# Moving the operands of SwiGLU to other offsets in on-chip memory

## The reference, cut to what matters

```
def swiglu(h, w1, w3, w2):            # h: 512 x 1024, w1 and w3: 1024 x 2816, w2: 2816 x 1024
    return (jax.nn.silu(h @ w1) * (h @ w3)) @ w2

for l in range(2):
    x = x + 0.5 * swiglu(rmsnorm(x, g_ffn1[l]), w1_a[l], w3_a[l], w2_a[l])
    x = x + mixers(rmsnorm(x, g_mix[l])) @ w_o[l]
    x = x + 0.5 * swiglu(rmsnorm(x, g_ffn2[l]), w1_b[l], w3_b[l], w2_b[l])
```

## Time and profile before

| | |
|---|---|
| median of three runs | 2801.64 us |
| the profiled execution's own time | 2803.92 us |
| its span, first to last instruction | 2801.9 us |
| TensorE matmuls busy | 2716.1 us (97%), 15,816 matmuls |
| TensorE weight loads busy | 2181.3 us (78%) |
| VectorE busy | 1774.7 us (63%) |
| ScalarE busy | 1092.5 us (39%) |
| GpSimd busy | 416.2 us (15%) |
| mean granted TensorE clock | 0.991 |

### The profile page before, as it was taken

One profiled execution on the slowest core, in us unless ns is written; L12 is line 12 of the kernel. 1 busy time (PEld: TensorE's weight loads), 2 busy tenths in 40 slices (PEclk: granted clock), 3 DMA queues, 4 the chain that ended last, 5 costly groups with the idle time before them and its releaser, 6 DMA issues.

```text
span 2801.9 us, 40254 instructions
## 1 busy us (share of the span) xinstructions
PE 2716.1 (97%) x15816; PEld 2181.3 (78%) x15816; DVE 1774.7 (63%) x2645; ACT 1092.5 (39%) x1586; POOL 416.2 (15%) x464
## 2 busy tenths in 40 slices
PE   9998999889699999999999999999999999999998
PEld 6576343333399998888889999899998888899997
DVE  6635232222787776665588777986777655787775
ACT  6832110100454444332354444554444233354443
POOL 3211000000021111101131110311101111221111
PEclk9999999999899999999999999999999999999999
DMA  5146999999465643332345564456542333365651
GB/s 214 45 175 263 420 420 420 420 420 421 141 181 166 173 136 100 103 101 94 100 124 168 167 172 136 114 164 176 158 136 89 94 94 106 98 172 142 176 158 60
DMA packets 138176, 505.65 MB, mean 180 GB/s; under 512 B 17025, under 2 KB 17537, under 8 KB 113153
## 3 DMA queue, kind: packets, MB, share of 16 engines
q1 hardware_dynamic: 101952, 422.36, 40.4%
q0 software_dynamic: 34688, 73.42, 12.8%
q10 hardware_dynamic: 1344, 7.23, 0.6%
HBM read 502.95 MB, written 4.19 MB: 181 GB/s over the span
## 4 chain that ended last, share of the span: by engine, by line
PE 73%; DMA 14%; DVE 5%; issue 4%; ACT 2%; POOL 1%; SPq 0%; DVEq 0%; ACTq 0%; POOLq 0%
PE bank L658 22%; PE bank L656 22%; PE bank L657 22%; DMA raw_more<-in_moe 4%; DMA raw<-in_moe 3%; PE bank L804 3%; DMA raw_over<-in_moe 3%; PE bank L839 2%; DVE w_lo L1875 1%; DMA sums<-in_w_b 1%; ACT w_hi L1272 1%; PE bank L662 1%; DMA raw<-in_w_b 1%; DVE ft L2289 0%; DMA x_rows<-x_tok 0%
## 5 line engine op out<-in xcount | busy, mean ns | idle before, releaser
L1875 DVE TENSOR_TENSOR w_lo<-raw,w_hi 128x1024 fp32r<-128x1024 f32 (+1 forms) x346 | 434.6, 1269 | 272.2 <-ACT w_hi L1272 265.7
L656 PE MATMUL bank<-xf_hi,w_lo 128*128 128x256 f32 x2112 | 590.1, 279 | 17.2 <-DVE w_lo L1875 9.6
L658 PE MATMUL bank<-xf_hi,w_hi 128*128 128x256 f32 x2112 | 585.3, 277 | 0.0
L657 PE MATMUL bank<-xf_lo,w_hi 128*128 128x256 f32 x2112 | 585.2, 277 | 0.0
L1272 ACT ACTIVATE w_hi<-raw 128x1024 fp32r<-128x1024 f32 (+1 forms) x356 | 366.0, 1039 | 273.9 <-PE bank L658 247.3
L656 PEld LDWEIGHTS bank<-xf_hi,w_lo 128*128 128x128 f32 x2112 | 397.6, 188 | 27.2 <-issue 14.1
L657 PEld LDWEIGHTS bank<-xf_lo,w_hi 128*128 128x128 f32 x2112 | 397.6, 188 | 2.4 <-issue 1.0
L658 PEld LDWEIGHTS bank<-xf_hi,w_hi 128*128 128x128 f32 x2112 | 397.4, 188 | 0.0
L658 PE MATMUL bank<-g_hi,w_hi 128*128 128x512 f32 x832 | 327.4, 394 | 0.0
L657 PE MATMUL bank<-g_lo,w_hi 128*128 128x512 f32 x832 | 326.2, 392 | 0.0
L656 PE MATMUL bank<-g_hi,w_lo 128*128 128x512 f32 x832 | 323.5, 389 | 0.3 <-DVE g_lo L2331 0.3
(11 more groups left out here) (367 smaller groups left out, 4549.0 us busy)
## 6 DMA issues: line engine op xcount, KB each, us to landing
raw_more<-in_moe SPq DMA_DIRECT2D x96, 1024.0 KB, 26.5
raw_over<-in_moe SPq DMA_DIRECT2D x48, 1024.0 KB, 27.4
raw<-in_w_a SPq DMA_DIRECT2D x77, 512.0 KB, 6.1
raw<-in_w_b SPq DMA_DIRECT2D x76, 512.0 KB, 6.3
raw<-in_w_in SPq DMA_DIRECT2D x73, 512.0 KB, 3.6
raw_top<-in_moe SPq DMA_DIRECT2D x24, 1024.0 KB, 27.9
raw<-in_moe SPq DMA_DIRECT2D x24, 1024.0 KB, 28.6
sums<-in_w_a POOLq DMA_DIRECT2D x88, 256.0 KB, 4.9
```

Of the source, the lines that this page charges most:

```text
L656: e.matmul(out, a_lo, b_hi, start=start, stop=False, skip_group_check=partial)
L657: e.matmul(out, a_hi, b_lo, start=False, stop=False, skip_group_check=partial)
L658: return e.matmul(out, a_hi, b_hi, start=False, stop=stop, skip_group_check=partial)
L1875: e.tensor_tensor(lo, source_of(k), hi.bitcast(F32), ALU.subtract).then_inc(s["lo"], 1)
```

## The change

Three pads of 16 values become 64 values, and the pads that follow shrink so that everything else stays where it was. `g` and `xf` move up by 192 bytes, from 192 to 384 past a multiple of 512. `pad_e` is moved from ahead of `e_hi` to behind `e_lo`, so that `e` moves down by 64 bytes, from 192 to 128. `raw_late`, `xT`, `rsq`, `sums`, `uu`, `snap`, `vv`, `ft` and the mixer's own buffers stay. No instruction, wait or DMA is added, removed or reordered, and only start addresses differ.

```
-        sb("pad_g", [P, 16])
+        sb("pad_g", [P, 64])
         g_hi = sb("g_hi", [P, 8, T], F32R)
         g_lo = sb("g_lo", [P, 8, T], F32R)
-        sb("pad_late", [P, 112])
+        sb("pad_late", [P, 64])
...
-            sb("pad_xf", [P, 16], into=ffn)
+            sb("pad_xf", [P, 64], into=ffn)
             xf_hi = sb("xf_hi", [P, KH, 7 * HALF], F32R, ffn)
             xf_lo = sb("xf_lo", [P, KH, 7 * HALF], F32R, ffn)
-            sb("pad_sums", [P, 112], into=ffn)
+            sb("pad_sums", [P, 64], into=ffn)
             sums = sb("sums", [P, 2, W], into=ffn)
-            sb("pad_e", [P, 16], into=ffn)
             e_hi = sb("e_hi", [P, 2, T], F32R, ffn)
             e_lo = sb("e_lo", [P, 2, T], F32R, ffn)
+            sb("pad_e", [P, 16], into=ffn)
```

## The result

| | before | after |
|---|---|---|
| median | 2802.47 us (4 runs) | 2831.15 us (2829.40 to 2836.56, 4 runs) |
| the profiled execution's own time | 2803.92 us | 2829.82 us |
| its span | 2801.9 us | 2828.0 us |
| TensorE matmuls busy | 2716.1 us | 2744.3 us |
| VectorE busy | 1774.7 us | 1775.7 us |

The change made the kernel slower: the ratio is 1.0105, with a 95% interval of 1.0092 to 1.0118. The forecast was faster, 2787 us. The range 2755 to 2842 held the time, and rival 1 had named both the place and the price (2834 us).

What follows compares the result with a forecast made beforehand. TensorE was taken to bound the kernel, fully busy inside each SwiGLU. Terms -7.0 (e), -2.4 (xf over w) and -5.6 (g) sum to -15.0 us, 2803.92 to 2788.9, median about 2787 us; range 2755 to 2842.

Steps and rivals of the forecast that it cites:

- rival 1: Long part of every SwiGLU: distance 256 acts as distance 0, xf over w at 120, +31.9, 2834 us; chance 0.24.
- What bounds the kernel: TensorE is 73% of the chain of waits and busy 240.00 of 240.00 us inside a SwiGLU.
- Its full number: Inside a SwiGLU, a nanosecond on every matmul moves the end by its full number.
- That the pace depends on where the operands lie: Matmuls differing only in operands differ in length (277 against 283 ns); each loses 6.7 to 18.5 ns, set by distance.
- (b): xf over w, 6336 SwiGLU matmuls, goes from distance 64 to 256: -2.4 us taken, worst row +37.5.
- I take the best row: For xf over w at distance 256: all matmuls at 113.3 ns, 4.8 us saved, half of it counted.
- the rule of one meeting and one quantum: Far-apart streams meet a weight load only once, costing 6.67 ns; distances 0 and minus 64 show two quanta.
- (a): xf over e, 1056 matmuls, goes from distance 0 to 256: 120.0 to 113.3 ns, -7.0 us.
- The sum: Whole kernel: -7.0 - 2.4 - 5.6 = -15.0 us.
- (c): g, 2496 matmuls of 512 columns, goes from distance 64 to 256: best row 226.7 ns, -5.6 us.
- (d): ScalarE and VectorE use moved tiles at other offsets: 0; mixer pieces of w over g: under 1 us.
- The 17% in a second regime: 426 of 2464 matmuls on xf_lo, in the first tens of us of each SwiGLU, at 117.8 ns.

Runs made afterwards that it cites:

- w_192: Against the kernel before, only the weights w_hi and w_lo moved from 128 to 192 (params, consts and ones shift 64 bytes too); 2850.65 us, one run.
- e_128: Against the kernel before, only e moved, from 192 to 128, with xf and g left at 192; 2814.61 us over ten runs, ratio 1.0036.
- g_128: Against the kernel before, only g moved, from 192 to 128 (distance 0 over w), xf and e left at 192; 2815.79 us, ratio 1.0040.

## Why the prediction was wrong

**What bounds the kernel** was right in the main, and no other engine took over. "Its full number" was too much: of 32.8 us by the paces, 26.1 came out in the span, and 6.8 went into shorter pauses.

**That the pace depends on where the operands lie, and on their distance,** was right, and w_192 shows it. By the rule of the Trainium skill, "SBUF — State Buffer", section "SBUF: two separate sides", that TensorE never waits on anyone, nothing should have moved. The traces don't agree: with xf itself unmoved, shifting only the weights took its matmuls from 277 to 284 ns in length, and their pace from 114.1 to 120.0.

**(b) is the step that failed.** "I take the best row", with the reason that streams which start far apart can meet only once. It gave -2.4 us and measured +37.4. Distance 256 is not far apart, it is distance 0 again. The rows that the rule of one meeting and one quantum was read from had one wrong distance as well: the earlier trace rows is at minus 56, and 192, the true minus 64 by the period, was later measured at 117.8. Rival 1 gave 120.0 ns, +37.5 us, the condition and the place, and each was measured so. The weight I put on the earlier trace rows against it was wrong: 2 ns between a transpose and a product told nothing, since products at 256 and at 0 both take 120.0. What the rows of before did offer was that distance 0 and minus 56 cost 120, and that a change from the one cheap distance had more to lose (37 us) than to win (5 us). I named that and gave it too little.

**(a)** gave -7.0 us and measured +0.1. The reason, that xf must cost over e what it costs over w, was right: both are 120.0. With (b) wrong it brought nothing.

**The sum** was -15.0 us, and the medians differ by +28.7. (b) alone is 39.8 us of the 43.7 between them.

**(c)** gave -5.6 us, "by the same reasoning as in (b)", and measured -4.7. That the size came out was luck: it was the return to distance 0, not a meeting far out. The earlier trace rows is 696 ns for three by the finer starts, 232 each, in place of 231.8, which changes nothing.

**(d)** was right: the stretches show VectorE and ScalarE as before, and the mixer keeps its pace. The distances of w over g are not minus 64 and minus 256 for all pieces, for the reason given for the earlier trace rows, but the term stays under 1 us.

**The 17% in a second regime** The earlier trace rows were taken as a nuisance of 2.4 us. The earlier trace rows counts all matmuls on xf_lo in four stretches, over e and in the fast regime too; the starts of the whole trace give 17% all the same (1006 of 5960 threes). They were the sign of what e_128 and g_128 showed: at distance 64 the pace is 113.3 or 117.8 by what went before. The price in (a) of moving e alone would have been wrong as well: not -7.0 but +8.8 us by the paces.

That the loss comes from the weight load and the moving stream meeting in SBUF is still argued, not shown. The runs show that their distance counts, not what they do to one another. A matmul without a weight load beside it was not tried.

## What to carry to other kernels

Two operands that TensorE reads at the same time should be laid out by their distance and not by their addresses. Measure distance modulo the period before taking "far" for "free": here 256 of 512 was the same as none. One step from a point that is already the cheapest known has little to win, so the prior belongs with the rows that are dear. And where a pace has two regimes, an operand that looks dear on its own may be what keeps the others in the cheap one, so price it with its neighbours.

## What the runs showed of the hardware that was not expected

- The pace of an fp32r matmul depends on the distance between its moving operand and the weights, and for the distances tried it repeats every 256 bytes. With 256 columns it is 120.0 ns at 0 and 256, 113.3 or 117.8 at 64 and 320 (117.8 alone for w over pf in w_192), and 117.3 to 119.9 at 32, 48, 96, 128 and 192. With 512 columns it is 226.7 at 0 and 256, 228.9 or 232.7 at 64, and 233 to 234 at 32, 96, 160 and 192, with 232 for the few of pp at 128.
- At distance 64 the pace depends on history and can then last for over 200 us (e_128, 1512.9 to 1769.9 us). One kernel's ten runs spread from 2805.41 to 2829.39 us. Within a stretch of xf over w it changed only where a start came late, 25 times in seven traces.
- Going from e back to w under the same xf led to the fast regime in 36 of 41 cases, going from g at 128 to xf at 192 to the slow one in 34 of 34.
- At distances 0 and 64 the losses are near multiples of 16 columns at 2.4 GHz: three matmuls of 256 columns take 340.0, 353.3 or 360.0 ns, which is 48, 80 or 96 columns over 768. At 32, 48 and 96 other lengths occur (346 to 365 ns).
